# Post-norm of block 1 taken apart by token tile, and residual transposes in the order of the residual adds

## The reference, cut to what matters

```python
def rmsnorm(x, g):
    return xf * rsqrt(mean(xf * xf, -1) + EPS) * g

h = h + rmsnorm(m @ w_out, norm_mix_post)        # after the mixers
u2 = rmsnorm(h, norm_mlp_pre)
a = square(relu(u2 @ w_up))
h = h + rmsnorm(a @ w_down, norm_mlp_post)       # after the MLP
```

## Time and profile before

| | us |
|---|---|
| median of 3 runs | 1547.61 (1547.23 to 1548.56) |
| the profiled execution | 1547.14 |
| its span, first to last instruction | 1545.3 |
| PE busy / weight load busy | 1525.1 / 1338.9 |
| DVE, ACT, POOL busy | 971.2, 757.7, 49.0 |
| mean granted TensorE clock | 0.996 of full speed |

### The profile page before, as it was taken

How to read it: one execution, slowest core, us unless ns; L and a number is a source line. 1 busy time by engine, 2 the same in 40 slices (tenths; PEclk the granted TensorE clock), 3 DMA queues, 4 the chain that set the end, 5 groups by cost and what they waited for, 6 DMA issues and landing times.

```text
span 1545.3 us, 22608 instructions
## 1 busy us (share of the span) xinstructions
PE 1525.1 (99%) x8738; PEld 1338.9 (87%) x8738; DVE 971.2 (63%) x1008; ACT 757.7 (49%) x839; POOL 49.0 (3%) x77
## 2 busy tenths in 40 slices
PE   9999999999999999999999999999999999999997
PEld 7888888888888899989888888888899989888886
DVE  5557766557666665766666656666666666576665
ACT  5544544446444454545544445444445444464444
POOL 0210000000000000000100000000000000000000
PEclk9999999999999999999999999999999999999999
DMA  9545455554554464343455554555545344255552
GB/s 369 193 144 184 155 200 183 198 190 181 195 194 178 176 214 167 127 174 137 163 180 195 176 195 179 191 190 190 190 179 203 120 173 174 107 191 190 190 190 109
DMA packets 39639, 279.54 MB, mean 181 GB/s; under 512 B 4368, under 2 KB 4624, under 8 KB 6160
## 3 DMA queue, kind: packets, MB, share of 16 engines
q1 hardware_dynamic: 38848, 275.27, 49.5%
q10 hardware_dynamic: 720, 3.29, 0.6%
HBM read 277.49 MB, written 1.05 MB: 180 GB/s over the span
## 4 chain that ended last, share of the span: by engine, by line
PE 97%; DVE 1%; ACT 0%; issue 0%; DMA 0%; POOL 0%; POOLq 0%; ACTq 0%; DVEq 0%
PE ps L351 95%; PE ps L538 1%; PE ps L568 0%; DMA res<-x_in 0%; DVE res L1456 0%; PE ps L861 0%; ACT xT L917 0%; DVE Pb L1436 0%; PE ps L547 0%; DVE PTb L1433 0%; PE ps L528 0%; POOL stat L1838 0%; DVE Vx L1403 0%; ACT scratch L1263 0%; ACT Vx L1266 0%
## 5 line engine op out<-in xcount | busy, mean ns | idle before, releaser
L1277 DVE TENSOR_TENSOR w_lo<-raw,w_hi 128x2048 fp32r<-128x2048 f32 x252 | 576.3, 2290 | 308.4 <-ACT w_hi L907 307.7
L907 ACT ACTIVATE w_hi<-raw 128x2048 fp32r<-128x2048 f32 x253 | 484.3, 1914 | 344.9 <-PE ps L351 333.6
L351 PE MATMUL ps<-xT,w_hi 128*128 128x512 f32 (+1 forms) x3016 | 651.4, 343 | 0.0
L351 PEld LDWEIGHTS ps<-xT,w_hi 128*128 128x128 f32 x3016 | 515.3, 191 | 57.2
L351 PE MATMUL ps<-xT,w_lo 128*128 128x256 f32 x2304 | 407.5, 283 | 0.0
L351 PEld LDWEIGHTS ps<-xT,w_lo 128*128 128x128 f32 x2304 | 346.7, 191 | 12.3
L351 PE MATMUL ps<-w_hi,sT_hi 128*128 128x512 f32 x576 | 185.7, 391 | 0.8 <-DVE Vx L1403 0.8
L351 PE MATMUL ps<-w_lo,sT_hi 128*128 128x512 f32 x576 | 184.9, 390 | 0.0
L351 PE MATMUL ps<-w_hi,sT_lo 128*128 128x512 f32 x576 | 184.7, 389 | 0.0
L351 PE MATMUL ps<-w_hi,xT 128*128 128x512 f32 x576 | 175.6, 393 | 0.2 <-ACT w_hi L985 0.2
L351 PEld LDWEIGHTS ps<-w_hi,xT 128*128 128x128 f32 x576 | 107.8, 188 | 24.7 <-issue 1.3
(11 more groups left out here) (167 smaller groups left out, 837.6 us busy)
## 6 DMA issues: line engine op xcount, KB each, us to landing
raw<-stream_in SPq DMA_DIRECT2D x256, 1024.0 KB, 4.8
kTx<-mem_in ACTq DMA_DIRECT2D x2, 1024.0 KB, 6.6
res<-x_in SPq DMA_DIRECT2D x2, 512.0 KB, 5.9
kTx<-mem_in SPq DMA_DIRECT2D x1, 1024.0 KB, 8.6
cu<-gate_bias_in SPq DMA_DIRECT2D x1, 1024.0 KB, 13.0
qk_tok<-post_gain_in ACTq DMA_DIRECT2D x1, 1024.0 KB, 5.0
out<-Vx SPq DMA_DIRECT2D x2, 512.0 KB, 3.1
cst<-consts_in SPq DMA_DIRECT2D x1, 512.0 KB, 7.1
```

Source lines behind the costliest of these rows:

```text
L351: return nc.tensor.matmul(bank_ap, lh, rh, start=start, stop=stop)
L907: nc.scalar.activation(w_hi[:, slot(c), 0:width], raw[:, slot(c), 0:width], copy).then_inc(unit_hi, 1)
L1277: nc.vector.tensor_tensor(w_lo[:, slot(c), :], raw[:, slot(c), :], w_hi[:, slot(c), :].bitcast(F32), sub).then_inc(unit_lo, 1)
```

## The change

It does five things.

1. ACT's squares of the post-norm products get `scale=D ** -0.5`, so that their sums are parts of a mean.
2. POOL's work for a post-norm, four operations of 128x2 after the last sum, becomes five: one of 128x2 that adds EPS to the two sums of half 0, and for each token tile an add and a power of 128x1. Tile 0 needs three of the four sums, tile 1 all four.
3. DVE interleaves: gain for q = 0, 1, 2; residual for q = 0; gain for q = 3; residual for q = 1, 2, 3. ACT's reload of the memory into `kTx`, which waited for all four gains (`postmlp`), waits for the last of them (`postmlpb`).
4. A new `turn_res` transposes `res` by half, then token tile, then four k, and waits for one quarter at a time. `turn_T` counts after tile 1 of each odd k. It is used after both post-norms (the second is FFN1 of the first layer) and at the start of every FFN in block 2. The transposes for the mixer and the cross attention keep `turn`.
5. `WARM_NORM` goes from 7 to 5.

```diff
-WARM_X, WARM_FIRST, WARM_NORM = 3, 3, 7
+WARM_X, WARM_FIRST, WARM_NORM = 3, 3, 5
...
+            def turn_res(banks, before):
+                for half in range(2):
+                    for t in range(TOK):
+                        pe.wait_ge(res_ready, before + 2 * half + t + 1)
+                        for k in range(4 * half, 4 * half + 4):
+                            last = nc.tensor.transpose(ps[:, banks[k // 2], (k % 2) * S + t * P:(k % 2) * S + (t + 1) * P],
+                                                       res[:, t, k * P:(k + 1) * P], ident)
+                            if t == 1 and k % 2 == 1:
+                                last.then_inc(turn_T, 1)
...
-            turn(res, U, wait=lambda k: pe.wait_ge(res_ready, 2 if k < 4 else 4))
+            turn_res(U, 0)
...
-                    turn(res, U, wait=lambda k: pe.wait_ge(res_ready, before - 2 if k < 4 else before))
+                    turn_res(U, before - 4)
...
-                    nc.scalar.activation(scratch[:, 0:512], ps[:, 4 + q, :], square,
+                    nc.scalar.activation(scratch[:, 0:512], ps[:, 4 + q, :], square, scale=D ** -0.5,
                                          accum_out=part[:, q:q + 1]).then_inc(sums, 1)
...
-                did1(last, name)
-                dve.wait_ge(rstd, rstd_done(stat_i))
-                wait_own1(name)
-                for q in range(4):
+                dve.wait_ge(gpost_in, 16)
+                scaled(0)
+                scaled(1)
+                did1(scaled(2), f"{name}a")
+                dve.wait_ge(post_rstd, post_done(n, 0))
+                wait_own1(f"{name}a")
+                onto(0)
+                did1(scaled(3), f"{name}b")
+                dve.wait_ge(post_rstd, post_done(n, 1))
+                onto(1)
+                onto(2)
+                wait_own1(f"{name}b")
+                onto(3)
...
+                both, done = stat[:, T_MIX, 0:2], 5 * n
+                pool.wait_ge(sums, before + 2)
+                nc.gpsimd.tensor_tensor(both, part[:, 0:2], consts2[:, 2, :], ALU.add).then_inc(post_rstd, 1)
+                pool.wait_ge(post_rstd, done + 1)
+                for t in range(TOK):
+                    mean, inv = stat[:, T_MIX, 2 + t:3 + t], rs(T_MIX, t)
+                    pool.wait_ge(sums, before + 3 + t)
+                    nc.gpsimd.tensor_tensor(mean, stat[:, T_MIX, t:t + 1], part[:, 2 + t:3 + t], ALU.add).then_inc(post_rstd, 1)
+                    pool.wait_ge(post_rstd, done + 2 * t + 2)
+                    nc.gpsimd.tensor_tensor(inv, mean, consts2[:, 3, 0:1], ALU.pow).then_inc(post_rstd, 1)
```

More of the change, by code:

```diff
@@ L75 @@
           "O1", "soft2", "gate2", "rinv2", "PT2", "O2", "soft3", "gate3", "rinv3", "PT3", "O3", "oT_lo",
-          "m1", "m2q0", "m2q1", "mh0", "m2q2", "m2q3", "mh1", "postmix", "postmlp"]
+          "m1", "m2q0", "m2q1", "mh0", "m2q2", "m2q3", "mh1", "postmixa", "postmixb", "postmlpa", "postmlpb"]
 L_PE = ["S0", "PT0", "PV0", "S1", "PT1", "PV1", "S2", "PT2", "PV2", "S3", "PT3", "PV3", "To", "ssq",
@@ L218, in program @@
         sel_ready = sem("sel_ready")
-        part_sum = sem("part_sum")
+        post_rstd = sem("post_rstd")
         cols_ready = sem("cols_ready")
@@ L232, in program @@
         l_pe, l_act, l_dve = Steps(sem("l_pe"), L_PE), Steps(sem("l_act"), L_ACT), Steps(sem("l_dve"), L_DVE)
-        ST_X, ST_MEM, ST_WOUT, ST_NORM1, ST_MLP, ST_LAYER = range(6)
+        ST_X, ST_MEM, ST_NORM1, ST_LAYER = range(4)
         ST_FFN1, ST_MIX, ST_ATT, ST_CONV, ST_XAT, ST_FFN2, NST = range(7)
@@ L240, in program, with post_done @@
         PER_LAYER_RES, PER_LAYER_TURN, PER_LAYER_QUARTERS, PER_LAYER_SUMS = 16, 6 * BT, 15, 10
+        def post_done(n, t):
+            return 5 * n + 2 * t + 3
         def rstd_done(i):
@@ L1159, in ffn @@
                     round_unit(L3, base + FFN + 1)
-                act.wait_ge(b_dve.sem, b_dve.upto("postmlp"))
+                act.wait_ge(b_dve.sem, b_dve.upto("postmlpb"))
                 act.dma_start(mem_tok, mem).then_inc(mem_in, 16)
@@ L1441, in _, with post_norm, scaled, onto @@
                 rest_unit(0, c)
-            def post_norm(stat_i, gain, name, before):
-                dve.wait_ge(gpost_in, 16)
-                for q in range(4):
-                    half, t = divmod(q, TOK)
+            def post_norm(n, gain, name, before):
+                def scaled(q):
+                    half = q // TOK
                     dve.wait_ge(sums, before + q + 1)
-                    last = nc.vector.tensor_tensor(Pb[:, q, :], ps[:, 4 + q, :], gain[:, half * 512:half * 512 + 512], mul)
-                did1(last, name)
-                dve.wait_ge(rstd, rstd_done(stat_i))
-                wait_own1(name)
-                for q in range(4):
+                    return nc.vector.tensor_tensor(Pb[:, q, :], ps[:, 4 + q, :], gain[:, half * 512:half * 512 + 512], mul)
+                def onto(q):
                     half, t = divmod(q, TOK)
@@ L1516, in _ @@
                     rest_unit(r * 4, c + 6)
-            post_norm(ST_MLP, gpost[:, D:2 * D], "postmlp", 10)
+            post_norm(1, gpost[:, D:2 * D], "postmlp", 10)
             b_dve.closed()
@@ L1857, in _, with post_statistic @@
                 last.then_inc(alibi_ready, 1)
[L1858 to L1863, removed]
+            def post_statistic(n, before):
+                both, done = stat[:, T_MIX, 0:2], 5 * n
[8 more added lines that the diff above has]
+                    nc.gpsimd.tensor_tensor(inv, mean, consts2[:, 3, 0:1], ALU.pow).then_inc(post_rstd, 1)
+            post_statistic(0, 4)
+            pool.wait_ge(sums, 10)
+            statistic(ST_NORM1, T_FFN, D)
+            post_statistic(1, 10)
             pool.wait_ge(cols_in, 16)
```

2 lines of the change are left out of this document (1 added, 1 removed).

## The result

The changed kernel took **1552.38 us** (median, 1551.23 to 1554.02) against 1546.86 of the kernel before in the same comparison (1545.78 to 1548.56): a ratio of 1.0036, 95% interval 1.0026 to 1.0046. It is 5.5 us slower. The forecast was 1544.1, its range 1543.2 to 1546.5.

A forecast was written before the change was run, and what follows sets the result against it. PE's matmul was taken as the bound (95% of the span), so only seams could gain: 1.38 + 1.18 - 0.5 + 1.4 = 3.46 us, off the median 1547.61, gave 1544.1, range 1543.2 to 1546.5.

The forecast's parts named there:

- the cut: Layer loop's return: instruction packets end at fixed program places, so fewer zeros let more PE work precede the stall; gain 1.4.

The follow-up runs named there:

- both cures: The changed kernel with the old order of transposes in FFN2 and DVE's wait for POOL's power in FFN1 only: 1542.63 us, and 1543.34 when repeated.

## What to carry to other kernels

Where one engine can hold another's operation for the whole of its own, as DVE's `w_lo` holds POOL's power here, a short operation on the path has a margin against the start of the long one next to it. List these margins before moving anything by a tenth of a microsecond: inside the margin a shift costs no more than its length, beyond it nearly the whole long operation. If the margin is thin, let the long operation wait for the short one, and only there: it cost 0.45 us at each FFN2 where it was not needed, and brought 7.4 us in the changed kernel, over all places together.

## What the runs showed of the hardware

- POOL's additions and powers are held alike by `w_lo`, and an addition by DVE's residual add (two SBUF operands) too: 0.38 instead of 0.19.
- The hold goes one way: a `w_lo` that began 0.13 to 0.48 behind a power took its 2.29 all the same.
- Independent POOL operations of 128x2 start 0.15 apart, dependent ones that wait on a semaphore 0.27; so one more of them may be nearly free (0.03).
- At the loop's return the instructions behind the cut arrived 4.8 to 6.0 us after the first transpose, whether 12 or 13 transposes, 16 and three matmuls, or 16 and eleven had been run by then. So work moved ahead of the cut is hidden. That the spread of 1.2 us in this arrival is a good part of the 3 us by which runs of one kernel differ is likely, but not shown: no kernel but the one with both cures was profiled twice (5.87 and 5.27 there).
